# A two-block transformer layer stack in fp32: norm roots as columns, a later state-space tail, an earlier low-rank fetch, and w_up's successor split by halves

## The chip, the cores and the metric

The kernel runs on one NeuronCore of a Trainium2 chip. The metric is the device time of one execution in microseconds (us), given as the median of several runs. The profile is one further execution, taken by the hardware profiler. Its engines are PE (TensorE, matrix multiplies; PEld is its weight load), DVE (VectorE), ACT (ScalarE), POOL (GpSimd) and SP (SyncE, which only issues transfers here). PE's granted clock is shown as a share of its full 2.4 GHz, so 1.00 is 2.4 GHz and 0.50 is 1.2 GHz.

## The reference, cut to what matters

One batch of 256 tokens with 2048 channels goes through two layers of a first block and one layer of a second, all in fp32:

```python
for l in range(2):                                    # first block
    shift, scale, gate = split(silu(c) @ w_ada[l] + b_ada[l], 3)
    h = rms_norm(x, norm_g[l]) * (1 + scale) + shift
    u, z_s, q, k, v, z_a = split(h @ w_in[l])
    y_s = s5_mixer(u, ...) * silu(z_s)                # state space scan, gelu, gated w_glu
    y_a = diff_attention(rope(q), rope(k), v) * silu(z_a)
    x = x + gate * (concat(y_s, y_a) @ w_out[l])
h = rms_norm(x, final_g)
z = rms_norm_2(h, pre_mix_norm) @ w_in                # second block
y_rw = rwkv7_mixer(z_rw, rw_w2, rw_a2, rw_g2, ...)    # these three are the low-rank matrices
y_mla = mla_mixer(z_mla, ...)
mix = (g_rw * (y_rw @ w_branch_rw) + g_mla * (y_mla @ w_branch_mla)) @ w_out
h = h + rms_norm_2(mix, post_mix_norm)
up = causal_dwconv(rms_norm_2(h, pre_ffn_norm) @ w_up, conv_w, conv_b)
f = (gelu(gate) * val) @ w_down
h = h + rms_norm_2(f, post_ffn_norm)
h = h + rms_norm_2(sigmoid(h @ w_ple_gate) * (p @ w_ple), ple_norm)
```

`rms_norm` divides each token by the root of the mean square of its 2048 channels.

## The kernel before, in words

**Layout.** Activations lie with channels on the 128 partitions and the 256 tokens along the free dimension, so `x` is 16 tiles of 128x256. A weight matrix is a row of column tiles of 128 output channels; one column tile is a chain of 128x128 blocks, `nk` of them (16 for 2048 input channels).

**Three multiplies for one.** Every fp32 value `a` is split in two: ACT writes a rounded `hi(a)` and DVE writes `lo = a - hi(a)`. A block of the stream is then three matmuls, hi by hi, hi by lo and lo by hi (`mm`). Weights come from memory in units of 128x2048 and are split by halves: `hi(p)` on ACT and `lo(p)` on DVE, 128x1024 each, serve eight blocks, that is 24 matmuls. Four split halves are held at a time (`NS`). Moving tiles are split too (`HT(k)` holds the pair of tile `k`); a matmul waits for its moving tile's `rhs` key.

**The order.** One `Timeline` is written out as a list of beats, and every engine plays the beats that concern it, in that order, with semaphore waits between engines. `stream` goes block by block through a matrix; every few blocks it lets each background generator (`bgs`) take one step: attention, the state-space scan (`s5`, `s5_back`), the adaptive modulation rows, the rwkv mixer. So the place of a background instruction on DVE or ACT is fixed by counting blocks, not by when its inputs are there, and every engine runs its own list strictly in order.

**State space.** `s5` runs 16 groups of 4; after group 7 the results of the first half are written to memory and read back transposed (`s5_y`, `s5_yr`), and `s5_out` then forms, for each of the four tiles of that half, the skip term and gelu: four DVE operations, a tanh on ACT, one DVE operation, and a hi and lo split. `s5_back` does this for half 0 while `w_in` is still being streamed, beside the attention of the middle heads, and for half 1 beside `w_outa`. The results are first used by `w_glu`, after `w_outa`. Column tiles 8 to 39 of `w_in` are the heads' q, k, v and gate, 40 to 47 the state-space gates (`z`).

**Norms.** A sum of squares stands as a 128x256 tile (`RS2`). One matmul with a 128x128 matrix of ones adds over partitions and repeats the sum on all of them (bank 3), ACT takes the root of 128x256, DVE the reciprocal of 128x256 (`RS`), and then every tile is multiplied by it. This is done between the two first layers (`("x", 0)`, then `h` for layer 1), after `w_out2` (tag `mo`, then `hf`), after `w_down1` (tag `fo`, then `xs`) and after `w_pg` (tag `em`, then the output). In `post`, DVE multiplies four tiles by `RS` and adds them to `x`, 128x1024 at a time. After `mo` the squares of the new `x` are taken by ACT (`sqf`) and added up by POOL, three additions of 128x1024.

**Low-rank matrices.** `rw_first` has ACT and DVE prepare the low-rank inputs and POOL then fetch the first set of matrices (`LW`) into an area that is free long before; PE's first low-rank matmul waits for that fetch.

**After w_up.** `w_ple` multiplies the second input `p`. Its two moving tiles take the places `HT(0)` and `HT(1)` of `w_up`'s moving tiles, so their split (`part("p", k)`) waits for the last matmul of `w_up`'s tile 87.

Of the kernel before, what the change touches and what calls it, by code (L numbers as in the profile page):

```python
# [100 lines left out]
N1, N2 = 25348, 11392  # L101
# [15 lines left out]
_c = Cursor(0)  # L117
RING = _c.alloc(NR * UNIT)
X = _c.alloc(4096)
# [27 lines left out]
QR, QI = _c.alloc(64), _c.alloc(64)  # L147
# [135 lines left out]
PAIRS = (("w_in", 48), ("w_in2", 0), ("w_up", 0), ("w_pg", 0))  # L283
# [11 lines left out]
class Timeline:  # L295
# [160 lines left out]
    def stream(self, name, l, u0, n0, nt, nk, per=8, late=None):  # L456
# [3 lines left out]
        for blk in range(nt * nk):  # L460
# [4 lines left out]
            if at % 16 == 0 and not ((name, u0) in PAIRS and blk < 16):  # L465
# [18 lines left out]
            if late is not None and blk == 39:  # L484
                late()
                late = None
# [66 lines left out]
    def s5_back(self, l):  # L553

        for half in range(2):
# [6 lines left out]
            for _ in range(8):  # L562
                yield
# [127 lines left out]

    def rms(self, tag, total):
        self.add("rms", tag, total)

    def run(self):
# [107 lines left out]
        for g in range(5):  # L803
            if g < 4:
                self.add("post", "mo", g)
            if g:
                for k in range(4 * g - 4, 4 * g):
                    self.add("hf", k)
                self.add("sqf", g - 1)
        self.add("ff_first")  # L810

# [7 lines left out]
        for k in range(2):  # L819
            self.add("part", "p", k)  # L820
# [5 lines left out]
        for g in range(5):  # L826
            if g < 4:
                self.add("post", "fo", g)
            if g:
                self.add("xs", g - 1)  # L830
# [3 lines left out]
        for g in range(4):  # L834
            self.add("post", "em", g)
# [191 lines left out]
def tensor_program(pe, m, tl, D):  # L1027
# [55 lines left out]
    def rms(tag, total):  # L1083
# [3 lines left out]
        pe.mm(B(3, 0, 256), con("ones"), V(RS2, 256), True, True).then_inc("norm_pe", tag)  # L1087

    def rmsf():
        pe.wait_ge("sum_pool", ("hf", 3))  # L1090
# [33 lines left out]
    def s5_run(l, b, i):  # L1124
        CC, VX, WI, CT, NST, ST, D0 = SETS[b % 2]
        u = lambda g: V(U8 + (4 * b + g) * 32, 32)
        if i == 0:
# [4 lines left out]
            else:  # L1132
                pe.wait_ge("norm_act", ("sqrt", ("x", 0) if l else "x0"))
# [268 lines left out]
    play = dict(mm=mm, ev=ev, mod=mod, modend=modend, sq=sq, rms=rms, rms2=rms2, rmsf=rmsf, lam=lam, s5_prep=s5_prep, s5_run=s5_run, att=att,  # L1402
# [23 lines left out]
def scalar_program(act, m, tl, D):  # L1426
# [33 lines left out]
    def rms(tag, total):  # L1460
        act.wait_ge("norm_pe", tag)
        act.act(V(RS, 256), B(3, 0, 256), ACT.Sqrt, bias=con("eps"), scale=1.0 / 2048).then_inc("norm_act", ("sqrt", tag))
# [42 lines left out]
    def part(tag, j):  # L1505
        to, src, key = parted(m, tag, j)
        free = {"yr": ("w_in2", 0, 67), "ya": ("w_brw", 0, 15), "mx": ("w_bmla", 0, 15), "p": ("w_up", 0, 87),
                "cq": ("w_in2", 0, 67)}
        if isinstance(tag, str) and (tag != "cq" or j >= 4):
# [283 lines left out]
    play = dict(begin=begin, hi=hi, modrow=modrow, sq=sq, rms=rms, rms2=rms2, rmsf=rmsf, h=h, hf=hf, sqf=sqf, xs=xs, lam=lam, tables=tables, part=part,  # L1793
# [18 lines left out]
def vector_program(dve, m, tl, D):  # L1812
# [55 lines left out]
    def recip(tag):  # L1868
        dve.wait_ge("norm_act", ("sqrt", tag))
        dve.recip(V(RS, 256), V(RS, 256))  # L1870
# [34 lines left out]
    def h(l, k):  # L1905
# [3 lines left out]
        for j in ([k] if k % 4 == 0 and l == 0 or k == 0 else []) + ([k + 1] if k < last else []):  # L1909
            dve.stt(V(UT + 256 * j, 256), V(X + 256 * j, 256), V(GP + j, 1), V(RS, 256), MUL, MUL).then_inc("h_dve", (l, j))  # L1910
# [335 lines left out]

    def post(tag, g):
        src, stream, sem = {"mo": (MO, "w_out2", "ev_act"), "fo": (FO, "w_down1", "g_act"), "em": (EM, "w_pg", "g_act")}[tag]
        t, x = V(src + 1024 * g, 4, 256), V(X + 1024 * g, 1024)
        dve.wait_ge(sem, ("ev", tl.out_of[stream, 0, 4 * g + 3].o))  # L2250
        dve.tt(t, t, V(RS, (0, 4), (1, 256)), MUL)
# [8 lines left out]
    def ev(t, ph):  # L2260
# [105 lines left out]
        elif t.kind == "pg":  # L2366
# [4 lines left out]
            if ph == 3:  # L2371
# [5 lines left out]
                mla=mla, post=post, ev=ev)  # L2377
# [8 lines left out]
def gpsimd_program(pool, m, tl, D):  # L2386
# [65 lines left out]
    def rw_first():  # L2452
        pool.wait_ge("rw_dve", "gd")
# [40 lines left out]

    def sqf(g):
        pool.wait_ge("norm_act", ("sqf", g))
        if g:
            if g > 1:
# [233 lines left out]
```

## Time and profile before

| | us |
|---|---|
| median of 3 runs | 3246.94 |
| lowest, highest | 3246.91, 3251.76 |
| profiled execution, its own time | 3253.76 |
| its span (first to last instruction) | 3252.0 |
| PE busy | 2995.8 |
| DVE busy | 2265.5 |
| ACT busy | 1624.1 |
| POOL busy | 334.0 |

The mean granted clock of PE over the execution is 0.96. In the views, a row names the line of the helper that issued the instruction (L910 is any DVE `tensor_tensor`, L920 any `scalar_tensor_tensor`, L950 any matmul, L947 any ACT operation), the tile written and the tile read, the shape, and how many instructions were merged. `rounded` and `upper_rounded` hold split values, `arena` and `upper` plain ones, `acc` the accumulation banks. One of the rounded 128x1024 rows is half a weight unit.

### The profile page before, as it was taken

What the parts mean: (1) busy time and instruction counts of PE and PEld (TensorE: products, weight loads), DVE (VectorE), ACT (ScalarE), POOL (GpSimd) and SP (SyncE); (2) the same over time, 40 slices, a digit from 0 to 9 for tenths busy, and PEclk for the clock granted to TensorE, in tenths of its full rate; (3) what the DMA queues carried; (4) which work ended last, traced back from release to release, by engine and by line L of the source; (5) the groups of instructions that cost most, each with busy time, mean ns of one, the idle gap of its engine ahead of it and who ended that gap; (6) DMA issues with size and microseconds to landing.
All of it is one profiled execution on the core that took longest, in us unless ns stands there. A gap on an engine that the chain in (4) does not pass through costs nothing.

```text
span 3252.0 us, 60643 instructions
## 1 busy us (share of the span) xinstructions
PE 2995.8 (92%) x24264; PEld 2768.1 (85%) x24264; DVE 2265.5 (70%) x3538; ACT 1624.1 (50%) x2409; POOL 334.0 (10%) x587
## 2 busy tenths in 40 slices
PE   6889989998988799999899999999799999999987
PEld 2677777887977789999798889989799999999987
DVE  6367777588788877775666566666688845887565
ACT  3335655355565554745334342545555544555454
POOL 0012322100123131300000000110100000000000
PEclk8899999998999899999999998999899999999989
DMA  9877766874645346555233333555355555555543
GB/s 372 290 241 239 242 207 214 282 276 138 184 134 155 103 151 204 177 175 171 91 102 106 101 112 100 166 159 187 127 172 184 183 188 177 185 184 169 187 145 115
DMA packets 168745, 577.01 MB, mean 177 GB/s; under 512 B 39760, under 2 KB 39792, under 8 KB 156048
## 3 DMA queue, kind: packets, MB, share of 16 engines
q1 hardware_dynamic: 146784, 525.40, 49.1%
q0 software_dynamic: 21104, 44.27, 4.6%
q8 instruction: 191, 3.13, 0.4%
q10 hardware_dynamic: 576, 3.47, 0.3%
q14 instruction: 90, 0.74, 0.1%
HBM read 546.83 MB, written 17.83 MB: 174 GB/s over the span
## 4 chain that ended last, share of the span: by engine, by line
PE 59%; DVE 25%; ACT 8%; DMA 4%; issue 3%; SPq 1%; DVEq 0%; ACTq 0%; POOL 0%
PE acc L950 58%; DVE arena L910 7%; DVE rounded L910 6%; ACT arena L947 4%; DVE arena L920 3%; ACT rounded L947 2%; DVE upper L910 2%; DVE upper L920 1%; ACT L947 1%; ACT upper L947 1%; DVE rounded L920 1%; PE acc L953 1%; SPq L906 1%; DMA arena<-in_w_ada 1%; DMA arena<-in_w_in 1%
## 5 line engine op out<-in xcount | busy, mean ns | idle before, releaser
L950 PE MATMUL acc<-rounded 128*128 128x256 f32 x14688 | 1941.2, 292 | 52.9 <-issue 30.3
L950 PEld LDWEIGHTS acc<-rounded 128*128 128x128 f32 x14688 | 1845.3, 196 | 137.8 <-issue 103.8
L910 DVE TENSOR_TENSOR rounded<-arena,rounded 128x1024 fp32r<-128x1024 f32 (+1 forms) x832 | 1003.9, 1207 | 311.7 <-ACT rounded L947 242.8
L947 ACT ACTIVATE rounded<-arena 128x1024 fp32r<-128x1024 f32 (+1 forms) x864 | 883.8, 1023 | 648.7 <-PE acc L950 449.1
L950 PEld LDWEIGHTS acc<-upper_rounded,rounded 128*128 128x128 f32 x4560 | 553.2, 193 | 25.8 <-issue 14.2
L950 PE MATMUL acc<-upper_rounded,rounded 128*128 128x256 f32 x4560 | 560.8, 285 | 9.6 <-DVE rounded L910 5.5
L947 ACT ACTIVATE arena<-arena 128x256 f32<-128x256 f32 (+4 forms) x477 | 252.9, 530 | 308.5 <-DVE arena L910 207.3
L950 PE MATMUL acc<-arena 128*32 128x512 f32 (+5 forms) x1622 | 250.3, 480 | 59.8 <-DVE arena L910 22.8
L910 DVE TENSOR_TENSOR arena<-arena 128x256 f32<-128x256 f32 (+5 forms) x471 | 258.6, 549 | 49.9 <-ACT arena L947 30.1
L910 DVE TENSOR_TENSOR arena<-acc,arena 128x256 f32<-128x256 f32 (+3 forms) x280 | 119.0, 425 | 204.0 <-PE acc L950 181.1
L920 DVE SCALAR_TENSOR_TENSOR arena<-arena 128x256 f32<-128x256 f32 (+5 forms) x461 | 205.6, 446 | 59.2 <-ACT arena L947 31.2
L947 ACT ACTIVATE arena<-acc 128x256 f32<-128x256 f32 (+4 forms) x285 | 119.6, 420 | 208.7 <-PE acc L950 188.5
L950 PEld LDWEIGHTS acc<-arena 128*32 128x32 f32 (+4 forms) x1622 | 113.9, 142 | 125.6 <-DMA arena<-in_w_ada 42.0
L950 PE MATMUL acc<-upper 128*128 128x128 f32 (+9 forms) x1632 | 198.6, 299 | 17.6 <-DVE upper L910 9.6
L950 PEld LDWEIGHTS acc<-upper 128*128 128x128 f32 (+4 forms) x1632 | 157.0, 169 | 41.2 <-DVE upper L910 12.4
L906 POOL DMA_DIRECT2D arena<-arena x256 | 130.5, 517 | 322.0 <-ACT arena L947 315.8
L947 ACT ACTIVATE upper<-acc 128x256 f32<-128x256 f32 (+4 forms) x176 | 88.2, 501 | 147.7 <-PE acc L950 103.8
L947 ACT ACTIVATE arena<-acc,arena 128x256 f32<-128x256 f32 (+1 forms) x152 | 65.4, 430 | 96.0 <-PE acc L950 87.4
L953 PE MATMUL acc<-arena 128*128 128x128 f32 x384 | 74.2, 288 | 36.5 <-ACT arena L947 30.9
L950 PE MATMUL acc<-upper,arena 64*64 64x64 f32 (+3 forms) x514 | 72.8, 335 | 34.5 <-ACT arena L947 12.8
L950 PEld LDWEIGHTS acc<-upper,arena 128*128 128x128 f32 (+2 forms) x514 | 50.3, 166 | 47.1 <-issue 15.1
L953 PEld LDWEIGHTS acc<-arena 128*128 128x128 f32 x384 | 46.3, 145 | 48.5 <-ACT arena L947 37.0
(91 smaller groups left out, 1194.3 us busy)
## 6 DMA issues: line engine op xcount, KB each, us to landing
arena<-in_w_in SPq DMA_DIRECT2D x328, 512.0 KB, 4.5
arena<-in_w_ada SPq DMA_DIRECT2D x88, 1024.0 KB, 5.2
arena<-in_w_up SPq DMA_DIRECT2D x176, 512.0 KB, 4.1
arena<-in_w_down SPq DMA_DIRECT2D x88, 512.0 KB, 4.1
arena<-in_w_outa SPq DMA_DIRECT2D x32, 512.0 KB, 6.0
arena<-in_w_glu SPq DMA_DIRECT2D x32, 512.0 KB, 6.2
arena<-in_w_outm SPq DMA_DIRECT2D x32, 512.0 KB, 4.6
arena<-in_w_out SPq DMA_DIRECT2D x32, 512.0 KB, 4.3
```

Source lines behind the costliest of these rows:

```text
L906: self.e.dma_start(out, in_).then_inc(self.signals.sems[sem], 16)
L910: return self.put(self.e and self.e.tensor_tensor(o, a, b, op))
L920: return self.put(self.e and self.e.scalar_tensor_tensor(out=o, in0=a, scalar=s, in1=b, op0=o1, op1=o2))
L947: return self.put(self.e and self.e.activation(o, a, f, scale=scale, **kw))
L950: return self.put(self.e and self.e.matmul(o, l, r, start=start, stop=stop, skip_group_check=True))
L953: return self.put(self.e and self.e.transpose(o, i, self.m.con("ident")))
```

## The change

Seven things change.

1. `s5_back` waits, before the outputs of half 0, until column tile 43 of `w_in` has been evicted, in both layers.
2. The first low-rank fetch is issued by POOL in `rw_zero` once the first column tile of `w_in2` is done.
3. The split of `p` for `w_ple` stands between the two halves of `w_up`'s tile 87 and waits only for the first of them.
4. For `("x", 0)`, `mo`, `fo` and `em` the ones are the moving operand: two matmuls of one column each give the sums as two 128x1 columns (`NCOL`). Root and reciprocal are of 128x2. PE then spreads each column over 128 tokens with an identity matmul into bank 3, and DVE reads the factor from there. The state-space scan, which uses bank 3 too, waits for layer 1's last `h` in place of the root.
5. `warm` takes a root of one column at the first block of tile 15 of `w_outm` (both layers), `w_out2` and `w_down1`.
6. `post` is cut in `scale` and `post`: the first tiles of the next matrix are split after one addition and two multiplications. The squares after `mo` are added by DVE, one addition at a time between weight halves (`sum4`), not by POOL.
7. The first four column tiles of `w_pg` are streamed four blocks of each in turn (`QUADS`), from a weight layout packed for it.

```diff
-PAIRS = (("w_in", 48), ("w_in2", 0), ("w_up", 0), ("w_pg", 0))
+PAIRS = (("w_in", 48), ("w_in2", 0), ("w_up", 0))
+QUADS = (("w_pg", 0),)
...
+            quads = (name, u0) in QUADS
+            if quads and blk < 64:
+                n, k = n0 + blk // 4 % 4, 4 * (blk // 16) + blk % 4
...
+                if (name, n, k) == ("w_up", 87, 8):
+                    self.spared = p
+                    for i in range(2):
+                        self.add("part", "p", i)
...
+            if (name, n, k) in (("w_outm", 15, 0), ("w_out2", 15, 0), ("w_down1", 15, 0)):
+                self.add("warm")
...
             for _ in range(8):
                 yield
+            while half == 0 and ("w_in", l, 43) not in self.marks:
+                yield
...
+    def scaled(self, tag, g):
+        if g == 0:
+            self.add("scale", tag, 0)
+        self.add("post", tag, g)
+        if g < 3:
+            self.add("scale", tag, g + 1)
+
+    def square_sums(self):
+        yield
+        for g in range(1, 4):
+            self.add("sum4", g)
+            yield
...
-        pe.mm(B(3, 0, 256), con("ones"), V(RS2, 256), True, True).then_inc("norm_pe", tag)
+        for th in range(2):
+            x = pe.mm(B(3, th, 1), V(RS2 + 128 * th, 128), con("ones", 1), True, True)
+        x.then_inc("norm_pe", tag)
+
+    def recip(tag):
+        if tag in ("x0", "hf"):
+            return
+        pe.wait_ge("norm_dve", ("col", tag))
+        for th in range(2):
+            x = pe.mm(B(3, 128 * th, 128), V(NCOL + th, (0, 128)), con("ident"), True, True)
+        x.then_inc("norm_pe", ("over", tag))
...
+            to, sums = V(NCOL, 2), B(3, 0, 2)
+        act.act(to, sums, ACT.Sqrt, bias=con("eps"), scale=1.0 / 2048).then_inc("norm_act", ("sqrt", tag))
+
+    def warm():
+        act.act(V(NCOL + 2, 1), con("eps"), ACT.Sqrt)
...
+        if tag == "p":
+            act.wait_ge("mm", ("half", tl.spared))
...
+            dve.recip(V(NCOL, 2), V(NCOL, 2)).then_inc("norm_dve", ("col", tag))
...
+    def sum4(g):
+        dve.wait_ge("norm_act", ("sqf", g))
+        dve.tt(V(AR, 1024), V(AR, 1024), V(AR + 1024 * g, 1024), ADD).then_inc("sum_dve", ("hf", g))
+
+    def scale(tag, g):
...
+        dve.wait_ge("norm_pe", ("over", tag))
+        dve.tt(t, t, B(3, 0, (0, 4), (1, 256)), MUL)
...
-    def rw_first():
-        pool.wait_ge("rw_dve", "gd")
+    def rw_zero():
+        pool.wait_ge("mm", ("out", tl.out_of["w_in2", 0, 0].o))
         pool.dma(V(LW, 384), D["lora"][0], "l_lw", 0)
```

How the instructions move is read from the order in which each engine's list stands. The line numbers shift by 23 between the two programs, so L910 before is L933 now, and L920 is L943.

First place: DVE in layer 0, beside the attention of a middle head. `upper<-upper,arena 128x256` and the three rows behind it are the first DVE part of `s5_out`, `upper<-arena,upper 128x256` is its second. Before:

```order
L910 TENSOR_TENSOR arena<-upper,arena 128x512 x2
L920 SCALAR_TENSOR_TENSOR upper<-upper,arena 128x256
L910 TENSOR_TENSOR arena<-upper 128x256
L916 TENSOR_SCALAR arena<-arena 128x256
L910 TENSOR_TENSOR arena<-arena,upper 128x256
L910 TENSOR_TENSOR arena<-arena 128x512
L910 TENSOR_TENSOR arena<-arena 128x576
L920 SCALAR_TENSOR_TENSOR upper<-arena,upper 128x256
L910 TENSOR_TENSOR rounded<-arena,rounded 128x1024
L910 TENSOR_TENSOR arena<-arena 128x576 x2
```

Now, at the same place:

```order
L933 TENSOR_TENSOR arena<-upper,arena 128x512 x2
L933 TENSOR_TENSOR arena<-arena 128x512
L933 TENSOR_TENSOR arena<-arena 128x576
L933 TENSOR_TENSOR rounded<-arena,rounded 128x1024
L933 TENSOR_TENSOR arena<-arena 128x576 x2
```

and among the last column tiles of the same `w_in`, where only weight halves and `z` evictions (`arena<-arena,acc`) stood:

```order
L933 TENSOR_TENSOR upper<-arena 128x4x31
L943 SCALAR_TENSOR_TENSOR upper<-upper,arena 128x256
L933 TENSOR_TENSOR arena<-upper 128x256
L939 TENSOR_SCALAR arena<-arena 128x256
L933 TENSOR_TENSOR arena<-arena,upper 128x256
L933 TENSOR_TENSOR rounded<-arena,rounded 128x1024
L943 SCALAR_TENSOR_TENSOR upper<-arena,upper 128x256
L943 SCALAR_TENSOR_TENSOR arena<-arena,acc 128x256
```

Four such groups leave the middle heads in each layer and stand among the last `z` tiles and the first `w_outa` tiles; nothing else moves on DVE there, and half 1 stands where it stood.

Second place: DVE between `w_out2` and `w_up`. Four `rounded<-arena,rounded 128x256` are the low parts of four moving tiles of `w_up`; the 128x1024 rows on `arena` are `post`, `scale` and the sums. Before:

```order
L928 RECIPROCAL arena<-arena 128x256
L910 TENSOR_TENSOR arena<-arena 128x1024 x4
L920 SCALAR_TENSOR_TENSOR rounded<-arena,rounded 128x256 x4
L910 TENSOR_TENSOR arena<-arena 128x1024 x2
L920 SCALAR_TENSOR_TENSOR rounded<-arena,rounded 128x256 x4
L910 TENSOR_TENSOR arena<-arena 128x1024 x2
L920 SCALAR_TENSOR_TENSOR rounded<-arena,rounded 128x256 x8
L910 TENSOR_TENSOR rounded<-arena,rounded 128x1024 x4
```

Now:

```order
L951 RECIPROCAL upper<-upper 128x2
L933 TENSOR_TENSOR arena<-arena,acc 128x1024
L933 TENSOR_TENSOR arena<-arena 128x1024
L933 TENSOR_TENSOR arena<-arena,acc 128x1024
L943 SCALAR_TENSOR_TENSOR rounded<-arena,rounded 128x256 x4
L933 TENSOR_TENSOR arena<-arena 128x1024
L933 TENSOR_TENSOR arena<-arena,acc 128x1024
L943 SCALAR_TENSOR_TENSOR rounded<-arena,rounded 128x256 x4
```

The first four low parts stand behind three 128x1024 operations, no longer four, and three further 128x1024 additions stand behind the sixteenth low part, each between two weight halves.

Third place: ACT at the end of layer 0. The two `arena<-arena 128x256` are the squares of the last two tiles of `x`, the three `128x2x128` the scan's sines. Before:

```order
L947 ACTIVATE rounded<-arena 128x1024
L947 ACT_TABLE_LOAD
L947 ACTIVATE arena<-arena 128x2x128 x3
L947 ACTIVATE arena<-arena 128x256 x2
L947 ACT_TABLE_LOAD
L947 ACTIVATE arena<-acc,arena 128x256
```

Now:

```order
L970 ACTIVATE rounded<-arena 128x1024
L970 ACT_TABLE_LOAD
L970 ACTIVATE upper<-arena 128x1
L970 ACT_TABLE_LOAD
L970 ACTIVATE arena<-arena 128x2x128 x3
L970 ACTIVATE arena<-arena 128x256 x2
L970 ACT_TABLE_LOAD
L970 ACTIVATE upper<-acc,arena 128x2
```

`warm` stands ahead of the sines here, so the table of the root is loaded twice: once for `warm`, once after the sines.

## Rows read from the trace of the kernel before

**Rows 1.** The page: busy time, share of the span, instructions of PE and DVE.
```profile
PE 2995.8 (92%) x24264; PEld 2768.1 (85%) x24264; DVE 2265.5 (70%) x3538; ACT 1624.1 (50%) x2409; POOL 334.0 (10%) x587
```

**Rows 2.** Busy time by stretches: stretch, length, engines' busy time (count), clock, DMA, GB/s.
```profile
311.00:392.00 81.00, 77.36 (x663) 63.41 (x661) 65.70 (x117) 49.16 (x91) 20.80 (x39) 1.00 0.70 234
392.00:483.00 91.00, 79.58 (x642) 65.63 (x640) 71.86 (x132) 47.20 (x93) 24.37 (x43) 0.94 0.66 219
...
956.00:1032.00 76.00, 65.75 (x547) 59.20 (x544) 62.63 (x111) 46.47 (x86) 16.98 (x34) 0.96 0.43 132
1032.00:1122.00 90.00, 73.79 (x584) 66.04 (x582) 73.47 (x133) 46.95 (x92) 25.68 (x47) 0.91 0.43 128
1200.00:1240.00 40.00, 39.84 (x355) 38.06 (x354) 25.28 (x37) 17.64 (x24) 13.13 (x23) 1.00 0.61 184
```

**Rows 3.** PE in order of time: start, length, operation, count, idle before and releaser.
```profile
459.30 1.08 PE L950 MATMUL acc<-arena,upper 128*32 128x128 f32 x16 [5.25 <-DVE upper L910]
...
1101.30 1.08 PE L950 MATMUL acc<-arena,upper 128*32 128x128 f32 x16 [4.90 <-DVE upper L910]
```

**Rows 4.** PE, DVE and ACT in order of time, between layer 0 and layer 1.
```profile
780.21 1.22 PE L950 MATMUL acc<-arena 128*128 128x256 f32 x2 [4.72 <-DVE arena L910]
786.24 14.12 PE L950 MATMUL acc<-rounded 128*128 128x256 f32 x63 [4.81 <-issue]
...
775.38 1.28 ACT L947 ACT_TABLE_LOAD   x1
776.67 3.02 ACT L947 ACTIVATE arena<-arena 128x256 f32<-128x256 f32 x5
...
781.97 1.75 DVE L928 RECIPROCAL arena<-arena 128x256 f32<-128x256 f32 x1 [0.49 <-ACT arena L947]
```

**Rows 5.** PE in order of time, from w_out2 to w_up.
```profile
2326.51 2.90 PE L950 MATMUL acc<-rounded 128*128 128x256 f32 x12 [8.80 <-issue]
2333.32 2.29 PE L950 MATMUL acc<-rounded 128*128 128x256 f32 x9 [3.91 <-DVE rounded L920]
```

**Rows 6.** DVE in order of time in the same stretch, then POOL.
```profile
2320.74 5.07 DVE L910 TENSOR_TENSOR arena<-arena 128x1024 f32<-128x1024 f32 x4
2325.92 2.27 DVE L920 SCALAR_TENSOR_TENSOR rounded<-arena,rounded 128x256 fp32r<-128x256 f32 x4
...
2330.13 2.85 POOL L910 TENSOR_TENSOR arena<-arena 128x1024 f32<-128x1024 f32 x1 [120.64 <-ACT arena L947]
```

**Rows 7.** Groups by line and shape, 2326 to 2350: count, busy, mean ns, idle before.
```profile
L920 DVE SCALAR_TENSOR_TENSOR rounded<-arena,rounded 128x256 fp32r<-128x256 f32 x16 | 13.8, 862 | 2.0 <-DVE rounded L920 0.5
```

**Rows 8.** PE in order of time, from w_down1 to w_pg.
```profile
3135.74 2.90 PE L950 MATMUL acc<-rounded 128*128 128x256 f32 x12 [9.57 <-issue]
3139.61 60.64 PE L950 MATMUL acc<-rounded 128*128 128x256 f32 x484 [0.98 <-DVE rounded L910]
```

**Rows 9.** PE at the start of w_ple, and the stretch behind it.
```profile
2983.63 13.60 PE L950 MATMUL acc<-rounded 128*128 128x256 f32 x96 [4.52 <-issue]
...
2984.00:2986.00 2.00, 2.00 (x11) 2.00 (x11) 1.79 (x3) 1.06 (x2) 0.00 (x0) 0.50 0.00 0
```

**Rows 10.** PE and POOL at the first low-rank matmuls, and a stretch behind.
```profile
1543.03 1.22 PE L950 MATMUL acc<-upper 64*128 64x256 f32 x4 [5.89 <-DMA upper<-in_lora]
...
1538.77 0.56 POOL L906 DMA_DIRECT2D upper<-in_lora  x1 [171.72 <-DVE upper L916]
...
1548.00:1550.00 2.00, 2.00 (x11) 2.00 (x11) 0.06 (x1) 0.00 (x0) 0.55 (x1) 0.50 0.18 66
```

**Rows 11.** The end of the program on DVE, in order of time.
```profile
3238.66 10.25 DVE L910 TENSOR_TENSOR arena<-arena 128x1024 f32<-128x1024 f32 x8
```

**Rows 12.** Small operations like the new ones: PE in time, then DVE's group.
```profile
1710.27 1.05 PE L950 MATMUL acc<-arena 128*128 128x1 f32 x8
...
1714.14 1.05 PE L950 MATMUL acc<-arena,upper 128*128 128x128 f32 x8
...
L928 DVE RECIPROCAL upper<-upper 128x2 f32<-128x2 f32 x8 | 1.3, 166 | 4.2 <-ACT upper L947 4.2
```

More of the change, by code:

```diff
@@ L483, in stream @@
                 held.append(t)
-            if late is not None and blk == 39:
+            if late is not None and blk == (71 if quads else 39):
                 late()
@@ L802, in run @@
         self.add("recip", "mo")
[L803 to L809, printed above, removed]
+        for g in range(4):
+            self.scaled("mo", g)
+            for k in range(4 * g, 4 * g + 4):
+                self.add("hf", k)
+            self.add("sqf", g)
         self.add("ff_first")
+        self.bgs.append(self.square_sums())
         def late():
@@ L818, in run @@
         self.stream("w_up", 0, 44, 44, 44, 16)
-        for k in range(2):
-            self.add("part", "p", k)
         self.stream("w_ple", 0, 0, 0, 16, 2)
@@ L825, in run @@
         self.add("recip", "fo")
[L826 to L830, printed above, removed]
+        for g in range(4):
+            self.scaled("fo", g)
+            self.add("xs", g)
         self.stream("w_pg", 0, 0, 0, 16, 16)
@@ L1132, in s5_run @@
             else:
-                pe.wait_ge("norm_act", ("sqrt", ("x", 0) if l else "x0"))
+                if l:
+                    pe.wait_ge("rhs", ("h", 1, 15))
+                else:
+                    pe.wait_ge("norm_act", ("sqrt", "x0"))
                 pe.wait_ge("lam_act", 0)
@@ L1461, in rms @@
         act.wait_ge("norm_pe", tag)
-        act.act(V(RS, 256), B(3, 0, 256), ACT.Sqrt, bias=con("eps"), scale=1.0 / 2048).then_inc("norm_act", ("sqrt", tag))
+        if total is None:
+            to, sums = V(RS, 256), B(3, 0, 256)
+        else:
+            to, sums = V(NCOL, 2), B(3, 0, 2)
+        act.act(to, sums, ACT.Sqrt, bias=con("eps"), scale=1.0 / 2048).then_inc("norm_act", ("sqrt", tag))
+    def warm():
+        act.act(V(NCOL + 2, 1), con("eps"), ACT.Sqrt)
     def rms2():
@@ L1506, in part @@
         to, src, key = parted(m, tag, j)
-        free = {"yr": ("w_in2", 0, 67), "ya": ("w_brw", 0, 15), "mx": ("w_bmla", 0, 15), "p": ("w_up", 0, 87),
+        free = {"yr": ("w_in2", 0, 67), "ya": ("w_brw", 0, 15), "mx": ("w_bmla", 0, 15),
                 "cq": ("w_in2", 0, 67)}
-        if isinstance(tag, str) and (tag != "cq" or j >= 4):
+        if tag == "p":
+            act.wait_ge("mm", ("half", tl.spared))
+        elif isinstance(tag, str) and (tag != "cq" or j >= 4):
             act.wait_ge("mm", ("out", tl.out_of[free[tag]].o))
@@ L2674, in arrange @@
     order = np.concatenate([n, np.stack([16 + n, 24 + n, 32 + n, 40 + n], 1).reshape(-1), 8 + n])
-    A["w_in"] = np.concatenate([pack(w.reshape(2048, 48, 128)[:, order].reshape(2048, 6144)) for w in g["w_in"]])
+    A["w_in"] = np.concatenate([pack(w.reshape(2048, 48, 128)[:, order].reshape(2048, 6144))
+                                for w in g["w_in"]])
     A["w_outm"] = np.concatenate([pack(w[:1024]) for w in g["w_out"]])
```

48 lines of the change are left out of this document (26 added, 22 removed).

## The prediction

> **What bounds the kernel now.** I read the page's busy line first. PE works 2995.8 of 3252.0 us and DVE 2265.5 [rows 1], so a change pays only where PE stands still or runs at its lower clock. Then I read PE in order of time at each place that the change touches, and asked of every pause which engine ended it and what that engine had done just before. Last came the stretches by head pair, for the part of the change that moves work inside `w_in`. The pauses found are 5.25 and 4.90 us in attention, released by DVE [rows 3]; 4.72 and 4.81 between the layers [rows 4]; 8.80 and 3.91 after `w_out2` [rows 5]; 9.57 and 0.98 after `w_down1` [rows 8]; 4.52 ahead of `w_ple` [rows 9]; and 5.89 ahead of the low-rank matmuls, released by the fetch [rows 10]. A pause also costs clock: after it the granted clock is 0.50, the 1.2 GHz level, in which 12 matmuls of 128x256 take 2.90 us [rows 5], against 1.50 in the long run of 484 in 60.64 [rows 8]. The sum below is made against the profiled execution's own 3253.76 us; the median of runs is 6.8 lower, and I subtract the same gain from it.
>
> **G, the state-space tail.** The pair of heads that has the outputs of half 0 beside it takes 91 us in layer 0, the one before it 81. In layer 1 it is 90 against 76. DVE works 71.86 against 65.70 and 73.47 against 62.63, and the clock is 0.94 against 1.00 and 0.91 against 0.96 [rows 2]. The surplus is 10 + 14 = 24 us. What I can name of it: the two PE pauses, 5.25 + 4.90 = 10.2, in which the attention matmuls stand behind DVE operations that stand behind the outputs [rows 3], and the lower clock, 0.06 x 91 + 0.05 x 90 = 10.0. That is 20.2. In the new place, DVE works 25.28 of 40 us while PE works 39.84 at clock 1.00 [rows 2]: some 15 us are free, and four outputs cost DVE about 10.8 (73.47 less 62.63, the larger of the two differences), so they fit. I charge 0.5 per layer there, and leave 2 us of pause with the scan, whose matmuls and four-wide rows still stand in those heads. -20.2 + 1.0 + 2.0 = about -17. The ends are -24, the whole surplus, and -4, if the pauses belong to the scan's own chain and only the DVE time moved.
>
> **A, the low-rank fetch.** POOL issues it at 1538.77 and PE starts at 1543.03 after 5.89 us of idling [rows 10]. POOL had stood still for 171.72 us before that issue, so the matrices can be there more than 100 us earlier. Next latest are the low-rank inputs, which are ready before the fetch is issued. So the pause of 5.89 goes but for a few tenths. The clock is still 0.50 at 1548 to 1550 [rows 10], so some 7 us of work run at half speed behind that pause: another 2 to 4, since the pause would otherwise be followed by full speed only if nothing else waits. I take -8; ends -5.9 and -10. POOL's queue loses one issue there and gains it in that idle time.
>
> **F, the split of `p`.** The pause of 4.52 goes, if both hi and lo of `p` fit between the middle and the end of tile 87, 24 matmuls of some 3 us. The split is then late by a tenth or so at most. The clock of 0.50 behind it [rows 9] goes too, worth about 2. -6; ends -4.5 and -6.8. The waiting instruction is ACT's; what stands behind it there is the split of weight halves that are already three ahead, so nothing is late.
>
> **C, `w_out2` to `w_up`.** Before: sum matmul, root of 128x256, reciprocal (1.75, as in [rows 4]), four operations of 128x1024 in 5.07 (1.27 each), then the low part, and PE starts at 2326.51 [rows 5, 6]. Now the reciprocal is 0.17, but two matmuls and their semaphore stand behind it; eight small matmuls of this kind take 1.05 [rows 12], so two at half clock with the way between engines are about 1.0 in my estimate. That leaves about 1.1 of gain at the start with the shorter root, and the first low part stands behind three 128x1024, not four: 1.25 more. POOL's additions no longer run beside the low parts. These take 862 ns each in a group of 16 [rows 7] and 2.27 / 4 = 0.57 ahead of POOL's first addition [rows 6]; at 0.50 to 0.57 the sixteen would save 4.7 to 5.8. DVE gets the three additions, 3.7 us, but between weight halves. But PE at the lower clock needs 2.90 us for its 12 matmuls and 2.29 for the next 9 [rows 5], so it takes up part of the gain. I take -6.4; ends -10 (both pauses but 2.7) and -3 (only the start earlier and one tile's worth).
>
> **D, `w_down1` to `w_pg`.** About 1.4 from reciprocal and root, and 1.25 from the order, put PE's first matmul 2.7 earlier. Four blocks of four column tiles give 48 matmuls before the second group of moving tiles is wanted, so the pause of 0.98 [rows 8] goes, with some 0.2 of clock. The order of the weights asks for nothing new in total. -3.9; ends -5 and -2.
>
> **E, the end.** Eight operations of 128x1024 take the last 10.25 us [rows 11], unchanged. Reciprocal 1.75 to 0.17, less 1.0 for the spreading: -0.7; ends -1.3 and -0.4.
>
> **B, between the layers.** The early root ahead of the sines means a table load and one small root, 1.28 and about 0.3, ahead of the squares [rows 4]; the squares then end up to 1.5 later, and the table has to be loaded a second time as it is now. The gain is the reciprocal's 1.6, and the spreading takes back 1.0 to 1.2; some preparation on DVE that stood behind the reciprocal falls into the time of the root. Sum 0, ends -1 and +2. Layer 1's end and `w_in2` keep their form: 0. In `w_out2` and `w_down1` the early root lies beside 60 us of matmuls: 0.
>
> On that load the row says: 1.28 us, and the next ACT operation begins 0.01 behind it [rows 4]. By the Trainium skill, "ScalarE: Activation LUTs", section on what ACT_TABLE_LOAD costs, a switch costs the load of about 1283 ns and a drain of about 1380 besides. By it B would be an estimated 1.4 us more, and the result 3206.3; the trace shows the load alone, so the measurement decides.
>
> **The sum.** -17 - 8 - 6 - 6.4 - 3.9 - 0.7 + 0 = -42.0. 3253.76 - 42.0 = 3211.8 for the profiled execution; 3246.94 - 42.0 = 3204.9 for the median of runs, which I round to 3205.
>
> **Rivals.**
>
> *The surplus of those head pairs is the scan's, not the outputs'.* For it: the pauses are released by the scan's DVE step [rows 3], which stays, and DVE as a whole is only 79% busy there. Against it: DVE's queue is in order and the outputs stand before that step. Then G gives nothing to -4 and the rest stays: -25 - 0 to 4, about 3220 (3222 to 3218). Chance 0.22.
>
> *All the transitions pay in full and the clock with them.* G -22, A -10, F -6.7, C -8, D -4.5, E and B -1: -52, so 3195. For it: the clock column shows the lower level behind each pause. Against it: in C PE is itself slow while DVE catches up. Chance 0.2.
>
> *Slower: the outputs are exposed in their new place.* Every `z` eviction, weight half and output part is in one DVE queue; an output's second part waits for its tanh on ACT, which stands behind weight halves of ACT's own. If PE then runs out of split halves, each of the eight outputs costs 2.7 us (10.8 / 4) and about 2.1 us of half clock, as behind the pause of 4.52 [rows 9]: 8 x 4.8 = +39. With the -25 of the rest, +14: 3261. It needs PE pauses of 2.8 us and more at every output, while DVE has 15 of 40 us free there and four halves are held. It decides from about 3.1 us per output on (25 / 8). Chance 0.03.
>
> *The fetch or `p` stays late for another reason* (A or F nought): 3211 to 3213. Chance 0.13, inside the range.
>
> The forecast itself has 0.4; 0.02 is left for something that none of this names.
>
> **How the numbers follow.** The ends of the terms summed go from -17.8 to -58.1; with the rivals at 3195 and 3220 the range that leaves out 2 in 10 is 3191 to 3225. A difference under 0.2% (6.5 us) can't be told from none. Even the small ends together are -17.8, outside that. So slower is the slower rival's 0.03, same the unnamed 0.02, faster 0.95.
>
> **What would show it.** G: the two head pairs at 81 and 76 to 79 us, no PE pause near 5 us behind the scan's step, and no new pause among the last `z` tiles. A: no PE idle released by the fetch, clock 1.00 there. F: no pause ahead of `w_ple`. C: PE's first matmul 10 to 11 us behind the sum matmuls, sixteen low parts at about 0.5 us each. D: PE idle 6.9 instead of 9.57, and none after 12 matmuls. E: unchanged 10.25. B: one table load more, and both pauses about 4.7. I am wrong if the gain of A, F, C, D together is under 18, or if the two head pairs keep 90 us.

## The result, and the profile after

| | before | changed |
|---|---|---|
| median, us | 3249.35 (4 runs; the profiled one is not among them) | 3211.91 (4 runs, with the profiled one) |
| lowest, highest | 3246.91, 3256.39 | 3210.57, 3215.80 |
| profiled execution, its own time | 3253.76 | 3215.80 |
| span | 3252.0 | 3214.0 |

The ratio is 0.9873, with a 95% interval of 0.9853 to 0.9894. The forecast median was 3205, with a range of 3191 to 3225. The profiled execution is 38.0 us shorter, where the prediction had 42.0; its range is 22 to 56 below the median that it started from. The page of the changed kernel, the line that answers to [rows 1]:

```profile
PE 2987.0 (93%) x24288; PEld 2761.7 (86%) x24288; DVE 2256.7 (70%) x3541; ACT 1626.3 (51%) x2414; POOL 326.1 (10%) x584
```

PE is busy 8.8 us less with 24 matmuls more. Busy time counts slow matmuls as longer, so this is clock that came back; the other 29 us are pauses that went.

PE plays the same 19,248 matmuls on split operands in both kernels, so their count is a ruler. The table takes the time at which the n-th of them starts in each trace, and gives by how much the difference between the kernels grew in each piece. Minus is a gain of the changed kernel.

| matmuls | place | us | predicted |
|---|---|---|---|
| to 1440 | layer 0 up to the middle heads | +0.9 | no edit there |
| 1440 to 1920 | layer 0, middle heads | -16.6 | G, both layers: -18 |
| 1920 to 3072 | layer 0, later heads to the end of `w_glu` | +10.8 | G: +1 |
| 3072 to 3840 | `w_outm` and between the layers | -0.8 | B: 0 |
| 3840 to 4896 | layer 1, first heads | +0.3 | no edit there |
| 4896 to 5304 | layer 1, middle heads | -16.5 | G, in the -18 |
| 5304 to 5856 | layer 1, last heads, `z`, start of `w_outa` | +5.4 | G, in the +1 |
| 6912 to 7296 | behind layer 1, first tiles of `w_in2` | +1.6 | 0 |
| 8256 to 8352 | first low-rank matmuls | -9.2 | A: -8 |
| 8352 to 11904 | rwkv and mla | -1.8 | no edit there |
| 11904 to 12288 | `w_out2` to `w_up` | -5.3 | C: -6.4 |
| 14112 to 14400 | `w_up` to `w_down0` | -1.4 | no edit there |
| 17280 to 17700 | `w_ple` | -0.8 | F: -6 |
| 18432 to 18816 | `w_down1` to `w_pg` | -3.5 | D: -3.9 |
| behind the last | end | -1.1 | E: -0.7 |

The pieces left out are 0.0 each, and the sum is -38.0. Two things limit the reading. The kernel before has one profile only, and the pieces of layer 0 scatter: at matmul 1440, ahead of every edit, the profiles below stand at -0.9 to -5.2 where this one has +0.9. And the -0.8 between the layers isn't the norm's. From the last matmul of layer 0 (number 3455) to the first of layer 1 it is 11.14 us, where the kernel before has 11.04; the 0.8 comes from PE's waits for DVE within `w_outm`, where this profile gains 2.0 and loses 1.2. The head pairs by stretches, the same matmuls as in [rows 2]; columns are as there:

```profile
393.00:469.00 76.00, 75.40 (x644) 62.11 (x643) 62.10 (x109) 43.78 (x85) 24.65 (x44) 1.00 0.79 263
951.00:1027.00 76.00, 65.39 (x546) 59.01 (x545) 62.22 (x111) 45.87 (x86) 17.13 (x33) 0.96 0.42 132
1027.00:1101.00 74.00, 67.49 (x581) 60.14 (x579) 63.36 (x109) 43.37 (x84) 24.86 (x47) 1.00 0.52 154
```

76 us where 91 stood and 74 where 90 stood, at clock 1.00 for 0.94 and 0.91. DVE's work fell by 9.8 and 10.1, as the 10.8 of the prediction wanted. Of the pauses of [rows 3] there is one left in layer 1, at the same scan matmuls, of 0.53:

```profile
1082.89 0.65 PE L973 MATMUL acc<-arena,upper 128*32 128x128 f32 x16 [0.53 <-DVE upper L933]
```

**What was late next at `w_ple`.** PE in order of time, then ACT, for the stretch that answers to [rows 9]:

```profile
2939.75 9.64 PE L973 MATMUL acc<-rounded 128*128 128x256 f32 x79
2949.87 0.98 PE L973 MATMUL acc<-rounded 128*128 128x256 f32 x6 [0.48 <-DVE arena L933]
2954.17 9.66 PE L973 MATMUL acc<-rounded 128*128 128x256 f32 x66 [3.32 <-ACT arena L970]
```

```profile
2949.32 1.21 ACT L970 ACTIVATE arena<-arena 128x256 f32<-128x256 f32 x2 [3.62 <-DVE arena L933]
2952.05 0.42 ACT L970 ACTIVATE upper_rounded<-arena 128x256 fp32r<-128x256 f32 x1 [1.53 <-DVE arena L943]
2952.59 1.06 ACT L970 ACTIVATE rounded<-arena 128x1024 fp32r<-128x1024 f32 x1
2953.74 1.81 ACT L970 ACTIVATE arena<-acc 128x256 f32<-128x256 f32 x4
```

The pause of 4.52 is gone and `w_ple` starts 4.7 us earlier, measured against the end of `w_up`; twenty matmuls on, with the clock that came back, it is 6.6. A column tile of `w_ple` is only six matmuls and the stream has five banks here, one of them still `w_up`'s, so they are full soon after. Their evictions, `arena<-acc` at 2953.74, stand in ACT's list behind the gelu of `w_up`'s last tile, which waits for DVE's convolution. PE waits 3.32 for the first of them. Of the 6.6 gained, 5.8 us are lost within the next fifty matmuls: about 4 in the two pauses, the rest in the clock behind them.

**The norm after `w_out2`.** The sum matmuls of the kernel before, ahead of [rows 5]; then PE in order of time in the changed kernel, and DVE's group of low parts, for [rows 5] and [rows 7]:

```profile
2317.01 0.70 PE L950 MATMUL acc<-arena 128*128 128x256 f32 x2 [1.02 <-DVE arena L910]
```

```profile
2291.08 0.61 PE L973 MATMUL acc<-arena 128*128 128x1 f32 x4 [1.03 <-DVE arena L933]
2292.67 1.22 PE L973 MATMUL acc<-arena,upper 128*128 128x128 f32 x4 [0.99 <-DVE upper L951]
2298.49 2.90 PE L973 MATMUL acc<-rounded 128*128 128x256 f32 x12 [4.60 <-issue]
2303.39 7.68 PE L973 MATMUL acc<-rounded 128*128 128x256 f32 x48 [2.00 <-DVE rounded L943]
2312.78 5.46 PE L973 MATMUL acc<-rounded 128*128 128x256 f32 x29 [1.70 <-DVE rounded L943]
```

```profile
L943 DVE SCALAR_TENSOR_TENSOR rounded<-arena,rounded 128x256 fp32r<-128x256 f32 x16 | 7.8, 485 | 2.5 <-ACT rounded L970 1.0
```

From the first sum matmul to the first of `w_up` it is 7.4 us now and was 9.5 (2317.01 to 2326.51). The sixteen low parts take 485 ns each, where [rows 7] has 862. The sums and the spreading cost PE 0.61 and 1.22 us.

### The profile page after: what moved, and what is told of

It reads as the page before. It is cut to its first block, busy times and chain, and to the rows that moved or that the text cites. A ratio compares the mean times of both kernels' runs of the same rounds, so it can differ in the third digit from the quotient of the medians.

```text
span 3214.0 us, 60697 instructions
## 1 busy us (share of the span) xinstructions
PE 2987.0 (93%) x24288; PEld 2761.7 (86%) x24288; DVE 2256.7 (70%) x3541; ACT 1626.3 (51%) x2414; POOL 326.1 (10%) x584
## 4 chain that ended last, share of the span: by engine, by line
PE 63%; DVE 22%; ACT 8%; DMA 4%; issue 2%; SPq 1%; DVEq 0%; ACTq 0%; POOL 0%
PE acc L973 62%; DVE arena L933 7%; DVE rounded L933 5%; ACT arena L970 4%; ACT rounded L970 3%; DVE upper L933 2%; DVE arena L943 2%; DMA arena<-in_w_ada 1%; DVE upper L943 1%; PE acc L976 1%; ACT L970 1%; ACT upper L970 1%; DMA arena<-in_w_glu 1%; DMA arena<-in_w_outa 1%; SPq L929 1%
## 5 line engine op out<-in xcount | busy, mean ns | idle before, releaser
L933 DVE TENSOR_TENSOR rounded<-arena,rounded 128x1024 fp32r<-128x1024 f32 (+1 forms) x832 | 1003.8, 1206 | 302.5 <-ACT rounded L970 233.1
L973 PE MATMUL acc<-arena 128*32 128x512 f32 (+7 forms) x1630 | 248.9, 475 | 66.0 <-DMA arena<-in_w_ada 24.9
L933 DVE TENSOR_TENSOR arena<-arena 128x256 f32<-128x256 f32 (+5 forms) x462 | 247.5, 536 | 51.4 <-ACT arena L970 32.6
L933 DVE TENSOR_TENSOR arena<-acc,arena 128x256 f32<-128x256 f32 (+3 forms) x280 | 119.0, 425 | 195.7 <-PE acc L973 173.0
L943 DVE SCALAR_TENSOR_TENSOR arena<-arena 128x256 f32<-128x256 f32 (+5 forms) x461 | 205.6, 446 | 59.5 <-ACT arena L970 31.7
L929 POOL DMA_DIRECT2D scr_g<-arena x56 | 30.3, 543 | 554.1 <-ACT arena L970 280.0
```

What stands on the lines that cost most here:

```text
L929: self.e.dma_start(out, in_).then_inc(self.signals.sems[sem], 16)
L933: return self.put(self.e and self.e.tensor_tensor(o, a, b, op))
L943: return self.put(self.e and self.e.scalar_tensor_tensor(out=o, in0=a, scalar=s, in1=b, op0=o1, op1=o2))
L973: return self.put(self.e and self.e.matmul(o, l, r, start=start, stop=stop, skip_group_check=True))
```

## The experiments

All are edits of the changed kernel; each stage is read with the ruler of matmuls, against the one profile of the kernel before. `...` marks lines left out of an edit. Line numbers differ by one or two between them.

**The wait taken out (e1_no_wait).**

```diff
-            while half == 0 and ("w_in", l, 43) not in self.marks:
-                yield
```

> The changed kernel without its wait for column tile 43: the outputs of half 0 stand beside the middle heads again, in both layers. The theory: those outputs cost about 14 us in the heads of layer 0 and 16 to 17 in those of layer 1, and where they stand now about 8 and 5 to 6 come back, so the net is 5.6 + 10.9 = 16.5: about 3232 us in the profiled execution, 3228 as the median, and the two PE pauses of about 5 us behind the scan's DVE step are back. A rival, that the pauses belong to the scan itself and went for another reason: no more than 4 us slower than the changed kernel, and no such pauses.

Median 3230.16 us, ratio to the kernel before 0.9931 (0.9919 to 0.9944), against 0.9873 with the wait: 0.58% or 18.9 us, 18.3 by the medians. Profiled span 3229.7. The middle heads are at -0.7 and -0.2 against the kernel before. The two stretches, and the pauses that returned:

```profile
390.00:480.00 90.00, 79.69 (x640) 65.67 (x639) 71.27 (x131) 46.69 (x93) 24.66 (x43) 0.94 0.66 220
1032.00:1122.00 90.00, 73.51 (x586) 65.26 (x585) 73.85 (x133) 47.06 (x92) 25.88 (x48) 0.92 0.43 128
```

```profile
456.95 0.64 PE L971 MATMUL acc<-arena,upper 128*32 128x128 f32 x16 [3.77 <-DVE upper L931]
...
1101.59 1.08 PE L971 MATMUL acc<-arena,upper 128*32 128x128 f32 x16 [4.91 <-DVE upper L931]
```

So the surplus was the outputs', not the scan's: that rival of the prediction falls.

**Narrow outputs (e2_narrow).** In `s5_out` on DVE and ACT, for `j < 4`:

```diff
...
+            if j < 4:
+                yj, sj, uj = V(U8 + 256 * j, 16), V(GS, 16), V(UT + 256 * j, 16)
...
```

> The changed kernel with the outputs of half 0 formed for 16 of 256 columns only (five DVE operations and one tanh per tile 16 wide, in both layers); the rest of those tiles is left out. Their place stays. The theory, that the 8.6 us which layer 0 loses again behind the heads belong to weight transfers that PE now meets earlier: the lead over the kernel before at the end of layer 0 grows by 2 us at most (from 5 to at most 7), and in layer 1 by 2 to 3. The rival, that the outputs' own work on DVE and ACT costs it: the lead at the end of layer 0 is 11 to 13 us.

Span 3204.5. From matmul 1920 to 3072 it loses 7.2 against the kernel before. The lead at the end of layer 0 was 11.0, beyond the 7 that the theory gave, and by that number alone the rival would have it; but the lead at matmul 1440, ahead of every output, was already 2.5 larger. And a loss of 7.2 lies among those of the profiles with full outputs (2.1 to 10.8), so for layer 0 this run decides nothing. In layer 1 the piece from 5664 to 5856 fell from +3.1 to +0.2: there the outputs' own work costs 2.9 in its new place.

**Lighter transfers, with and without the wait (e3_cut, e4_cut_no_wait).**

```diff
+        if h is None and i >= 72:
+            sp.dma(V(ring_at(tl, item), UNIT // 4), w[:, :UNIT // 4], f"ring{tl.place[item]}", item)
```

> The changed kernel with the last 24 transfers of w_ada (those from about 540 us on) of a quarter of their bytes; the other three quarters of these units are left out. To be read against the next run, which has the same and no wait for tile 43. The theory, that in layer 0 the lead is lost to transfers: with them lighter the lead of this kernel over the next at the end of layer 0 is 10 us or more. The rival, that the outputs cost it in their new place: 5 to 6 us, as with full transfers.

> As the run before (the last 24 transfers of w_ada of a quarter of their bytes), without the wait for tile 43. It is the partner of that run: by the theory it reaches the end of layer 0 10 us or more later than that one, by the rival 5 to 6 us later. Both kernels should pass w_outa and w_glu of layer 0 faster than with full transfers; by the theory the one with the wait gains more by it.

Spans 3194.9 and 3218.9. At the end of layer 0 (3072) they lead the kernel before by 27.3 and 12.9, a difference of 14.4; at matmul 1920, behind the middle heads, it was 15.2 (18.7 and 3.5). So 0.8 of the wait's gain is lost there when transfers are light, and they pass the stretch 8.5 and 9.4 us faster than the kernel before, where the profiles with full transfers lose 2.1 to 10.8. That transfers limit this stretch is shown by that; how much of the lead they take is one pair of profiles against a scatter of 9 us. The DMA share there falls too, from 0.74 in the changed kernel, here the first row, to 0.56:

```profile
499.00:715.00 216.00, 197.49 (x1563) 167.54 (x1562) 151.67 (x274) 107.61 (x161) 31.56 (x56) 0.95 0.74 256
```

```profile
496.00:692.00 196.00, 189.21 (x1558) 159.70 (x1556) 148.61 (x265) 107.20 (x160) 31.14 (x55) 0.98 0.56 186
```

**Three edits undone (e5_undo_three).** In `rw_first`, the stream of `w_up`, and `PAIRS`:

```diff
-        pool.wait_ge("mm", ("out", tl.out_of["w_in2", 0, 0].o))
+        pool.wait_ge("rw_dve", "gd")
...
-            act.wait_ge("mm", ("half", tl.spared))
+            act.wait_ge("mm", ("out", tl.out_of["w_up", 0, 87].o))
...
-QUADS = (("w_pg", 0),)
+QUADS = ()
...
```

> The changed kernel with three edits undone that stand far apart and are read each at its own place: the low-rank fetch is issued late again, the split of p stands behind the whole of w_up's tile 87 again, and w_pg's first tiles go in pairs again, as w_up's do. The theory: the fetch costs 9 us at the first low-rank matmuls; the split of p costs only 0.8 to 1.5, because the 6 us that it gains at the start of w_ple are given back 4 us later, when PE waits for a bank that ACT can't evict yet; the pairs cost 0.5 to 1.5 in w_pg. Together 11 to 12 us more than the changed kernel's 3214.0. The prediction's working, as the rival: 8 for the fetch, 6 for p, 1.2 for w_pg, together 15.

At their places: 9.0 for the fetch, 0.8 for `p`, 0.5 for `w_pg`, 10.3 together. The pauses of 5.60 and 4.53 are back:

```profile
1516.23 1.23 PE L973 MATMUL acc<-upper 64*128 64x256 f32 x4 [5.60 <-DMA upper<-in_lora]
...
2946.92 13.34 PE L973 MATMUL acc<-rounded 128*128 128x256 f32 x94 [4.53 <-issue]
```

The span is 3211.7, 2.3 below the changed kernel's first profile and not 11 above it, as was expected: this execution was 11.4 ahead of that profile at the end of layer 0, where nothing had been edited. The expectation on the whole span was a miss, and the reason to run the changed kernel again.

**Sums on POOL (e6_pool_sums).**

```diff
-        self.bgs.append(self.square_sums())
...
+    def sqf(g):
+        pool.wait_ge("norm_act", ("sqf", g))
...
+            pool.tt(V(AR, 1024), V(AR, 1024), V(AR + 1024 * g, 1024), ADD).then_inc("sum_pool", ("hf", g))
```

> The changed kernel with the three additions of squares after mo on POOL again, at once behind the squares, in place of DVE's between weight halves. The theory, that POOL's additions slow the low parts that run beside them (862 ns each before, 0.56 now): the sixteen low parts take 3 to 5 us longer in all, and the lead at w_up's third column tile falls by 2 to 4 us. The rival, that the gain there came from the order of scale and post and from the norm alone: no loss, or a gain of up to 1 us from DVE's three additions going.

The piece 11904 to 12288 loses 3.4, inside the theory's 2 to 4. But the low parts take only 2.0 more together (9.8 against 7.8), not the expected 3 to 5. POOL makes three additions, and each cost DVE about 2 us on whatever stood beside it: an addition, three low parts (3.69 us, where they took 1.67 in the changed kernel), and three weight halves (5.61 for three of 1.23). The first of them, DVE and POOL in order of time:

```profile
2299.56 2.42 POOL L932 TENSOR_TENSOR arena<-arena 128x1024 f32<-128x1024 f32 x1 [121.25 <-ACT arena L969]
2299.78 3.28 DVE L932 TENSOR_TENSOR arena<-arena 128x1024 f32<-128x1024 f32 x1
2303.17 1.22 DVE L932 TENSOR_TENSOR arena<-arena,acc 128x1024 f32<-128x1024 f32 x1
```

DVE's first addition here began 0.22 behind POOL's and took 3.28 in place of 1.22. It ended 1.08 behind POOL's end, so it reads as held until POOL was done.

**No columns (e7_full_norm).** `rms`, `recip`, `scale` and `h` use 128x256 tiles again at all four places:

```diff
...
-            dve.recip(V(NCOL, 2), V(NCOL, 2)).then_inc("norm_dve", ("col", tag))
+        dve.recip(V(RS, 256), V(RS, 256))
...
-        dve.tt(t, t, B(3, 0, (0, 4), (1, 256)), MUL)
+        dve.tt(t, t, V(RS, (0, 4), (1, 256)), MUL)
```

> The changed kernel with the sums, roots and reciprocals of 128x256 again at all four places (no columns, no spreading matmuls); the early roots and the order of scale and post stay. By the two timelines the way from the sum matmul to the first operation that uses the factor is 2.9 us with columns, 3.2 expected without them where the table is loaded early: columns alone are worth 0.3 to 0.5 us after mo and after fo, 0.4 to 0.8 between the layers, and 0.6 to 0.8 at the end, where the table load stands in the way in both. Sum 1.6 to 2.6 us slower than the changed kernel. The rival, the prediction's 1.1 to 1.4 per place: 4 us or more.

Against the changed kernel: +1.5 between the layers (12.65 us from matmul 3455 to the next, for 11.14), 0.0 after `mo`, +0.8 after `fo`, +1.1 behind the last matmul. That is 3.4, above the expected 1.6 to 2.6 and under the rival's 4: the miss is mainly between the layers, where 0.4 to 0.8 was expected. Two pieces that the edit doesn't touch are slower too, by 1.0 (14112 to 14400) and 1.2 (`w_ple`), and still the span of 3214.8 is only 0.8 above the changed kernel's, since this execution was 4.6 ahead of that profile at the end of layer 0. The chain at `fo`:

```profile
3090.98 0.70 PE L973 MATMUL acc<-arena 128*128 128x256 f32 x2 [1.51 <-DVE arena L933]
...
3092.36 1.75 DVE L951 RECIPROCAL arena<-arena 128x256 f32<-128x256 f32 x1
3094.21 3.81 DVE L933 TENSOR_TENSOR arena<-arena 128x1024 f32<-128x1024 f32 x3
```

From the sum matmul to the first use of the factor it is 3.23 us here. In the changed kernel it is 2.41 after `fo` (3092.06 to 3094.47), and 2.90 after `mo`, where the four small spreading matmul records take 1.22 and not 0.71.

**A combined version (e8_combined), and both again (e9_after_again, e10_combined_again).**

```diff
-            if (name, n, k) in (("w_outm", 15, 0), ("w_out2", 15, 0), ("w_down1", 15, 0)):
+            if (name, n, k) in (("w_out2", 15, 0), ("w_down1", 15, 0)):
...
-        while self.pend:
+        while self.pend and not keep:
...
-        self.stream("w_up", 0, 44, 44, 44, 16)
+        self.stream("w_up", 0, 44, 44, 44, 16, keep=True)
```

> A version that follows from the traces: the changed kernel without the early root at the end of w_outm (in both layers), and with the evictions of w_up's last tile no longer drained before w_ple, so that ACT evicts the first three tiles of w_ple ahead of that tile's gelu. The theory: the early root costs 1.3 between the layers and 1.6 at the end of layer 1 (a PE pause of 1.63 behind the last low parts), and the bank wait of 3.3 at w_ple with its clock costs 4 to 5. So 6.5 to 8 us faster than the changed kernel: 3206 to 3208 in the profiled execution, 3204 to 3206 as the median. The rival, that at w_ple the weight halves are late as well: the pause there stays at 2 us or more and the gain is under 5 in all.

Median 3204.01, ratio 0.9837 (0.9817 to 0.9856), span 3202.8. Against the changed kernel: -1.5 between the layers and -1.6 at the start of `w_in2`, as expected; -2.6 at `w_ple`, below the expected 4 to 5; and +2.0 at `w_pg`, which was not expected. These stages give 3.7, so that the median is 7.9 lower, near the top of the expected 6.5 to 8, isn't their doing alone. PE and, below it, the clock at `w_pg` in this version:

```profile
3087.01 10.55 PE L973 MATMUL acc<-rounded 128*128 128x256 f32 x74 [5.33 <-issue]
3099.73 5.47 PE L973 MATMUL acc<-rounded 128*128 128x256 f32 x31 [2.17 <-DVE rounded L933]
```

```profile
3099.00:3103.00 4.00, 3.27 (x18) 3.27 (x19) 3.69 (x4) 1.50 (x2) 0.00 (x0) 0.69 0.51 150
```

The 74 matmuls took 10.55 us, in the changed kernel 11.46; PE then waited 2.17 instead of 1.26 for the same DVE rows, and behind the longer pause the clock fell once more. At `w_ple` the bank wait of 3.32 became two of 0.68 and 1.13:

```profile
2940.88 3.13 PE L973 MATMUL acc<-rounded 128*128 128x256 f32 x24 [0.68 <-ACT arena L970]
2945.15 5.12 PE L973 MATMUL acc<-rounded 128*128 128x256 f32 x39 [1.13 <-ACT arena L970]
```

> The changed kernel once more, unedited, timed on the same chip as the next run. It tells how much of a difference between two profiles is the run's own. The theory, that between the middle heads and the end of layer 0 the lead is set by the weight transfers and varies from run to run: the 10.8 us lost there in the first profile come out elsewhere between 4 and 8, while every stage from w_in2 on repeats within 0.5 us of the first profile. The rival, that the loss of 10.8 is the change's: 10 to 11 again. Median 3208 to 3214, ratio to the kernel before 0.985 to 0.989.

> The combined version once more (no early root at the end of w_outm, w_up's last tile not drained ahead of w_ple), on the same chip and with the same runs of the kernel before as the run ahead of it. The theory: 1.5 + 1.6 + 2.7 us gained at the three places, up to 2 us of it lost again at w_pg through the clock, so 4 to 6 us under the changed kernel's median on this chip, 0.12 to 0.19%. The rival, that the 10 us between the two medians so far were these edits: 9 us or more again.

On one chip: changed 3212.63 us, ratio 0.9873 (0.9851 to 0.9895); combined 3207.05, ratio 0.9847 (0.9825 to 0.9869). The difference of 5.6 us lies in the expected 4 to 6, but the two intervals overlap; that the combined version is the faster one is shown stage by stage (3.7 in the first pair of profiles), not yet by its total. In its second profile the changed kernel lost 2.1 us from matmul 1920 to 3072, not 10.8 (the expected 4 to 8 missed on the low side), and its span was 3206.7. From matmul 7296 on all its pieces repeat within 0.1 us, except that rwkv, from 8352 to 9984, is at -0.4 in place of -1.9. The first tiles of `w_in2` came out at +3.2 and not +1.6. So the expectation that every stage from `w_in2` on repeats within 0.5 missed at these two places.

## Why the prediction was right, point by point

**The total** was right for reasons that hold in part: -42.0 forecast, -38.0 in the profile, -37.4 by medians. A, C, D and F together gave 18.8, close to the 18 under which the prediction called itself wrong, and that G came out at -16.9 for -17 is luck.

**G, -17, was right in size; its parts were not.** The wait is worth 18 to 19 us. That the surplus is the outputs' and not the scan's is shown by e1_no_wait. But the heads gave 16.6 + 16.5 = 33, more than the whole surplus of 24 that the prediction set as its end: the pair with the outputs ended up faster than its neighbour (76 against 81 us), so a neighbour was not the floor. The step "I charge 0.5 per layer there" failed. In layer 1 the new place costs 2.9 (e2_narrow). The rest of layer 1's loss (5304 to 5664), 2.3 here, sits mostly at a wait of PE for the scan's DVE step. It comes out anywhere from -0.1 to 4.0 in the profiles with the wait, 4.0 with the outputs narrow, and at 0.0 and 4.9 in the two without it (e1_no_wait, e4_cut_no_wait), so it isn't the outputs' work; its cause stays open. In layer 0 the lead runs into a stretch that the weight transfers limit: in e3_cut and e4_cut_no_wait, with light ones, it is kept but for 0.8. How much of it is lost varies, from 2.1 to 10.8 in profiles with the wait and 4.2 in the one without. So what the wait is worth in layer 0 is 15 in the heads, and what is left of it at the end of the layer can't be given as one number from these runs: this profile leads the one without the wait by 6.1 there, e9_after_again by 17.0. In layer 1, from 3840 to 6912, the profiles with the wait and full transfers gain 7.4 to 10.9, the one without it 0.1. G's sum came out because its two errors, a gain of 33 for 18 and a loss of 16 for 1, cancel in this profile.

**A** was right: 9.0 to 9.2 for 8, pause and clock both. **D** was right: 3.5 for 3.9, though four column tiles in turn brought only 0.5 of it; the pause moved from the twelfth to the 74th matmul, and didn't go (1.26 for 0.98). **E**: 1.1 for 0.7.

**F failed.** The step was "what stands behind it there is the split of weight halves that are already three ahead, so nothing is late". The halves were ahead; the evictions behind them in the same list were not thought of. 6.6 gained, 5.8 lost, 0.8 left (e5_undo_three); in three other profiles with the edit the piece is at -0.2, -0.3 and +0.4, so even the 0.8 isn't firm. Moving the drain of one tile won back 2.6 (e8_combined).

**C** was right in size, 5.3 for 6.4. The start came 2.1 earlier for the 2.35 of the working; only the sign "PE's first matmul 10 to 11 us behind the sum matmuls" was misread, since that way was 9.5 before and is 7.4 now. Its largest part was the contention with POOL, 3.4 (e6_pool_sums). The columns, for which the prediction counted on the reciprocal's 1.6 less 1.0, brought 0.3 at the first matmul there and nothing by the end of the piece (e7_full_norm). A rule of the Trainium skill bears on this, "SBUF — State Buffer", section on two separate sides: a DVE operation with two inputs in SBUF, the on-chip memory, and one of GpSimd that reads it share a port pair, which the first to start holds for its whole instruction. The trace agrees for this pair of additions, 3.28 against 1.22 us; the prediction had read the same from the rows and had not needed it.

**B** came out at +0.1 for 0 at the norm itself, and for the stated reasons: the columns gain 1.5 and the early root costs 1.6. The way from matmul 3455 to the next is 11.04 us with neither (the kernel before), 9.54 with the columns alone (e8_combined), 12.65 with the early root alone (e7_full_norm) and 11.14 with both. The sign "both pauses about 4.7" doesn't hold: PE now waits 6.32 ahead of the sums, and 0.59 and 1.73 behind them. **The end of layer 1** failed as a step: the prediction has "Layer 1's end and `w_in2` keep their form: 0", but the early root stands there too, and costs 1.6. The early root's load and root, 1.28 + 0.30, stand ahead of the last squares and hi parts on ACT. The last low part on DVE and the weight halves behind it are late by as much, and PE waits for them:

```profile
1345.84 1.28 ACT L970 ACT_TABLE_LOAD   x1
1347.14 0.30 ACT L970 ACTIVATE upper<-arena 128x1 f32<-128x1 f32 x1
...
1353.31 6.85 PE L973 MATMUL acc<-rounded 128*128 128x256 f32 x55 [1.63 <-DVE rounded L933]
```

Without the early root PE runs through there, and no record of a wait stands there (e8_combined).

**What stays open.** The -1.4 from matmul 14112 to 14400 belongs to no edit. It is a wait of PE for DVE's weight half behind a convolution, 1.33 us in the kernel before and gone in the changed one. It is gone in every other run too, except e7_full_norm, the one without columns, where 0.99 is left; whether the columns have to do with it was not tested. Open too are what the other profiles show in the last heads of layer 1, and why layer 0 differs by up to 11 us between executions of one program.

## What to carry to other kernels

When a wait is removed, read the lists of the engines that serve the next stage to the depth of its buffers: not only the operands must be ready, the banks must be emptied, and the instruction that empties them may stand behind a slow tail. A background operation on a loaded in-order engine costs more than its own time where matmuls wait behind it: here 10 us of DVE work cost PE 15. And two profiles of a program are compared at counts of matmuls, not by span; otherwise 11 us of run-to-run change in one stage hide an edit worth 9 in another.

## What the runs showed of the hardware

- A table load took 1.28 us and the next ACT operation began 0.01 to 0.02 us behind it, at 1345.84 as at the rows shown ahead of the prediction.
- A DVE addition of 128x1024 took 3.28 us beside a POOL addition of the same size and 1.22 alone. The next DVE operation, with one operand in the accumulation banks, was not tested beside POOL.
- The lower clock makes gains uneven. The same four spreading matmul records took 1.22 us after `mo` and 0.71 after `fo`; and at `w_pg` a pause of 2.17 in place of 1.26, with the clock at 0.69 behind it, went with a loss of 2.0.
